# Query heads paired across key heads, and the fourth layer's rotary exchange by transfers inside SBUF

## The reference

```
def rope(x, pos):
    ...
    x1, x2 = jnp.split(xf, 2, axis=-1)
    return jnp.concatenate([x1 * cos - x2 * sin, x2 * cos + x1 * sin], axis=-1).astype(x.dtype)

def swa_mixer(h, w_in, sinks, w_o):
    W, hd, Hq, Hkv = SWA_WINDOW, HEAD_DIM, SWA_Q_HEADS, SWA_KV_HEADS     # 128, 64, 16, 4
    q, k, v = jnp.split(h @ w_in, [Hq * hd, (Hq + Hkv) * hd], axis=-1)
    q, k = rope(q), rope(k)                                               # heads split, positions 0..255
    # query head i uses key head i // 4; a band of 128 keys; a sink column in the softmax
    scores = where(mask, q k^T * hd ** -0.5, -inf)
    probs = softmax([scores, sink])[..., :-1]
    return (probs @ v) @ w_o
```

## Time and profile before

| what | value |
|---|---|
| median of 3 runs | 1587.19 us (1586.34 to 1588.76) |
| profiled execution, its own time | 1587.09 us |
| its span, first to last instruction | 1585.2 us |
| mean granted TensorE clock | 0.992 of full speed |
| layer 4's stage from the first unit pair's end to out_part(7) | about 989 to 1050 us of the span |

### The profile page before, as it was taken

One profiled execution on the slowest core, in us unless ns is written; L12 is line 12 of the kernel. 1 busy time (PEld: TensorE's weight loads), 2 busy tenths in 40 slices (PEclk: granted clock), 3 DMA queues, 4 the chain that ended last, 5 costly groups with the idle time before them and its releaser, 6 DMA issues.

```text
span 1585.2 us, 24605 instructions
## 1 busy us (share of the span) xinstructions
PE 1523.4 (96%) x9396; PEld 1320.1 (83%) x9396; DVE 1202.2 (76%) x1724; ACT 794.6 (50%) x1053; POOL 110.9 (7%) x111
## 2 busy tenths in 40 slices
PE   2989999999999999999999999999999999999999
PEld 1867888889988888899888888787888888889998
DVE  6898877778578777865687777968777788676666
ACT  2455444356464343565543445565434577655544
POOL 0150000000000000011000000220000063200000
PEclk8999999999999999999999999999999999999999
DMA  9855987856258878573478885446888655345550
GB/s 389 360 189 214 370 318 302 307 189 238 81 213 325 331 297 340 197 260 133 160 315 332 307 332 197 148 158 256 338 322 314 230 174 185 119 161 185 185 185 27
DMA packets 54908, 383.78 MB, mean 242 GB/s; under 512 B 6420, under 2 KB 6932, under 8 KB 9264
## 3 DMA queue, kind: packets, MB, share of 16 engines
q1 hardware_dynamic: 50976, 363.75, 60.9%
q0 software_dynamic: 3856, 18.97, 3.4%
HBM read 381.62 MB, written 4.22 MB: 243 GB/s over the span
## 4 chain that ended last, share of the span: by engine, by line
PE 81%; DVE 10%; DMA 3%; issue 3%; ACT 2%; POOL 1%; SPq 0%; DVEq 0%; ACTq 0%
PE PS L2367 27%; PE PS L1977 25%; PE PS L2425 17%; DVE adar L1423 3%; PE PS L1998 3%; DVE wlo L1398 2%; DMA CST<-cst_in 1%; PE PS L2128 1%; PE PS L2178 1%; PE PS L2403 1%; ACT whi L947 1%; DMA adar<-ada 1%; DVE SCR L1585 1%; PE PS L2056 1%; PE PS L2155 1%
## 5 line engine op out<-in xcount | busy, mean ns | idle before, releaser
L1398 DVE TENSOR_TENSOR wlo<-raw,whi 128x2048 fp32r<-128x2048 f32 x229 | 526.4, 2300 | 220.9 <-ACT whi L947 220.6
L947 ACT ACTIVATE whi<-raw 128x2048 fp32r<-128x2048 f32 x234 | 446.3, 1910 | 193.3 <-PE PS L2425 122.6
L1977 PE MATMUL PS<-hhi,whi 128*128 128x256 f32 x1104 | 320.6, 290 | 3.5 <-DVE wlo L1398 2.6
L1977 PE MATMUL PS<-hlo,whi 128*128 128x256 f32 x1104 | 314.5, 285 | 0.0
L1977 PE MATMUL PS<-hhi,wlo 128*128 128x256 f32 x1104 | 314.3, 285 | 0.0
L1423 DVE CUSTOM_DVE_ANT_0 adar<-adar,CB 128x1024 f32<-128x1024 f32 x232 | 277.0, 1234 | 8.4 <-DMA adar<-ada 8.3
L2367 PE MATMUL PS<-whi,hhi 128*128 128x512 f32 x704 | 278.5, 396 | 2.0 <-ACT hhi L996 2.0
L2367 PE MATMUL PS<-wlo,hhi 128*128 128x512 f32 x704 | 274.4, 390 | 0.0
L2367 PE MATMUL PS<-whi,hlo 128*128 128x512 f32 x704 | 274.1, 390 | 0.0
L1977 PEld LDWEIGHTS PS<-hhi,whi 128*128 128x128 f32 x1104 | 213.5, 193 | 11.3 <-issue 7.8
L1977 PEld LDWEIGHTS PS<-hlo,whi 128*128 128x128 f32 x1104 | 213.7, 194 | 1.6 <-issue 1.2
(11 more groups left out here) (259 smaller groups left out, 1993.3 us busy)
## 6 DMA issues: line engine op xcount, KB each, us to landing
raw<-weights SPq DMA_DIRECT2D x234, 1024.0 KB, 6.4
adar<-ada SPq DMA_DIRECT2D x104, 1024.0 KB, 6.2
adar<-ada POOLq DMA_DIRECT2D x12, 1024.0 KB, 5.5
raw<-ada SPq DMA_DIRECT2D x4, 1024.0 KB, 15.1
bias_rows<-bias_of_distance POOLq DMA_DIRECT2D x1, 3072.0 KB, 13.9
adar<-bias_rows POOLq DMA_DIRECT2D x8, 256.0 KB, 3.3
CST<-cst_in SPq DMA_DIRECT2D x1, 1128.0 KB, 22.7
CB<-c_in SPq DMA_DIRECT2D x2, 512.0 KB, 4.0
```

The lines of the kernel that those rows point to most:

```text
L947: act.activation(whi[:, u % CV, :], raw[:, u % RAW, :], ACT.Copy).then_inc(hi_done, 1)
L1398: v.tensor_tensor(wlo[:, u % CV, :], raw[:, u % RAW, :], whi[:, u % CV, :].bitcast(F32), ALU.subtract).then_inc(lo_done, 1)
L1977: m = pe.matmul(o, w(a), h(b), start=first and k_ == 0, stop=last and k_ == 2, skip_group_check=True)
```

## The change

1. The 16 query heads are paired across key heads: pair p holds the heads 8 (p // 4) + p % 4 and that + 4, which belong to the key heads 2 (p // 4) and 2 (p // 4) + 1. The columns of w_in, the rows of w_o and the sinks are put in that order on the host. So a half of the partitions meets only the key head that lies there, and the exchanged copy of KT (L1546) is dropped in both swa layers.
2. In layer 4 alone, the five products with the permutation matrix are dropped. In their place POOL issues, for each rotated unit, four transfers from SCR to the part of KT that has become free (columns 2 to 5, two buffers), each of 32 partitions x 512 elements (64 KB): the partition blocks exchanged two by two. DVE's rotation waits for them, and multiplies and adds in SBUF.
3. values(0) to values(2) of layer 4 no longer wait for rotations 3 to 5, since those products no longer write a bank that values use.

The core of the diff:

```diff
+def swa_heads():
+
+    return [8 * (p // 4) + 4 * h + p % 4 for p in range(PAIRS) for h in range(2)]
...
+        def moved_rotation(kind, l):
+
+            return kind == "swa" and l > 0
...
+        def partners(k):
+
+            return KT[:, 2 + 2 * (k % 2):4 + 2 * (k % 2), :].rearrange("p a b -> p (a b)")
...
+                def load_partners(i):
+
+                    k = aux_units[kind].index(i)
+                    pool.wait_ge(bank_read, reads[l, i])
+                    if k >= 2:
+                        pool.wait_ge(aux_done, aux0[l] + k - 1)
+                    for q in range(4):
+                        dst, source = 32 * q, 32 * (q ^ 1)
+                        pool.dma_start(partners(k)[dst:dst + 32, :], SCR[source:source + 32, k % 2, :]).then_inc(pair_in[k % 2], 16)
...
+                if moved_rotation(kind, l):
+                    for i in (0, 1, 3):
+                        load_partners(i)
                 if kind in ("swa", "fox"):
                     for p in range(PAIRS):
+                        if moved_rotation(kind, l) and p in (1, 2):
+                            load_partners(3 + p)
                         normalise(p)
...
-                    turned = two(SCR[:, 2, :])
-                    v.wait_ge(aux_pe, a + 1)
-                    v.tensor_tensor(rt, rt, bc(cst("cos", S), 2), ALU.mult)
-                    link(v.tensor_tensor(turned, two(aux_bank(kind, k)[:]), bc(cst("sin", S), 2), ALU.mult))
-                    if i:
-                        q = k - 1
-                        v.tensor_tensor(QT[:, 2 * q:2 * q + 2, :], rt, turned, ALU.add).then_inc(aux_done, 1)
+                    if moved_rotation(kind, l):
+                        turned = two(partners(k))
+                        v.wait_ge(pair_in[k % 2], 64 * (k // 2 + 1))
+                        v.tensor_tensor(rt, rt, bc(cst("cos", S), 2), ALU.mult)
+                        link(v.tensor_tensor(turned, turned, bc(cst("sin", S), 2), ALU.mult))
                     else:
-
-                        v.tensor_tensor(KT[:, 0:2, :], rt, turned, ALU.add)
-                        for half in range(2):
-                            other = slice(64 - 64 * half, 128 - 64 * half)
-                            e = v.tensor_tensor(KT[64 * half:64 * half + 64, 2:4, :], rt[other], turned[other], ALU.add)
-                        e.then_inc(aux_done, 1)
+                        turned = two(SCR[:, 2, :])
+                        v.wait_ge(aux_pe, pe0[l] + k + 1)
+                        v.tensor_tensor(rt, rt, bc(cst("cos", S), 2), ALU.mult)
+                        link(v.tensor_tensor(turned, two(aux_bank(kind, k)[:]), bc(cst("sin", S), 2), ALU.mult))
+                    dst = QT[:, 2 * k - 2:2 * k, :] if k else KT[:, 0:2, :]
+                    v.tensor_tensor(dst, rt, turned, ALU.add).then_inc(aux_done, 1)
                     v.wait_ge(aux_done, a + 1)
...
                 def aux_product(i):
 
+                    if moved_rotation(kind, l):
+                        return
...
-                            kt = p // 4 + 2 * ((p // 2 + h) % 2) if kind == "swa" else p
+                            kt = p // 4 if kind == "swa" else p
...
-                        if p < 3:
+                        if p < 3 and not moved_rotation(kind, l):
                             pe.wait_ge(aux_done, aux0[l] + 3 + p)
...
-                                col = HD * (p // 2 if kind == "swa" else 2 * p + h)
+                                col = HD * (2 * (p // 4) + h if kind == "swa" else 2 * p + h)
```

More of the change, by code:

```diff
@@ L233, in program @@
         bank_read = sem("projection_read")
+        pair_in = [sem(f"rotation_partners_loaded{i}") for i in range(2)]
         aux_in, aux_pe, aux_roots, aux_done = sem("aux_squares"), sem("aux_product"), sem("aux_roots"), sem("aux_done")
@@ L324, in program @@
         aux_units = {"swa": [0, 1, 3, 4, 5], "b2": [0, 1, 3, 4, 6, 7, 9, 10]}
-        aux0, total = {}, 0
+        aux0, pe0, total, products = {}, {}, 0, 0
         for l, k in enumerate(kinds):
-            aux0[l] = total
+            aux0[l], pe0[l] = total, products
             total += len(aux_units.get(k, []))
+            products += 0 if moved_rotation(k, l) else len(aux_units.get(k, []))
+        def partners(k):
+            return KT[:, 2 + 2 * (k % 2):4 + 2 * (k % 2), :].rearrange("p a b -> p (a b)")
         def aux_bank(kind, a):
@@ L1043, in square_read @@
                     if k >= 2:
-                        act.wait_ge(aux_pe, aux0[l] + k - 1)
+                        act.wait_ge(aux_pe, pe0[l] + k - 1)
                     act.wait_ge(pe_unit, u0 + i + 1)
@@ L1050, in head_root @@
                     k = aux.index(i)
-                    act.wait_ge(aux_pe, aux0[l] + k + 1)
+                    act.wait_ge(aux_pe, pe0[l] + k + 1)
                     if k >= 2:
@@ L2544, in pack @@
             gains += [i["norm_gain"][src, 0], i["norm_gain"][src, 1]]
+            if kind == "swa":
+                w_in, w_o = w_in.copy(), w_o.reshape(16, HD, D)[swa_heads()].reshape(D, D)
+                w_in[:, 0:D] = w_in[:, 0:D].reshape(D, 16, HD)[:, swa_heads()].reshape(D, D)
         units += [cols(w_in, UC * n, UC) for n in UNIT_ORDER[kind]]
@@ L2575, in pack @@
     put("lam", np.stack([i[n][0] for n in ("lambda_q1_2", "lambda_k1_2", "lambda_q2_2", "lambda_k2_2")], 1), HD)
-    put("sinks", np.broadcast_to(i["swa_sinks"].reshape(1, 32), (P, 32)))
+    put("sinks", np.broadcast_to(i["swa_sinks"][:, swa_heads()].reshape(1, 32), (P, 32)))
     put("bf", i["fox_b_f"][0][:, None], 16)
```

## The result

The changed kernel takes **1601.54 us** (median of 4 runs, 1600.20 to 1602.82), the kernel before 1587.03 beside it (4 runs): a ratio of **1.0089** (95% interval 1.0077 to 1.0101), 14.5 us slower. The forecast was 1592.9, range 1588.8 to 1598.8. The direction was right, the size was not, and the time lies outside the range.

The account below looks back on a forecast made before the run. PE and DVE, both full in layer 4, were taken to bound the kernel. Layer 4's +7.1 and layer 1's -1.4 made +5.7 us, forecasting 1592.9 us, with a range of 1588.8 to 1598.8.

Parts of the forecast that it names:

- What bounds the kernel: Layer 4: PE and DVE are both full, so taking work from PE alone gains nothing while DVE stays late.
- Layer 1, -1.4: Layer 1, first rotation: dropping its two half copies saves 1.4 us, or 0 if DVE meets a late load.
- Layer 4, the first two rotations, +0.9: Layer 4 before scores(0): DVE waits for two groups of transfers, landing 2.7 us after issue, so scores(0) comes 0.9 later.
- The bound of 6.0: Layer 4's first two rotations: slowest transfer landing assumed, 6.0 us, which would put scores(0) 4.2 us later.
- The rule that I drew from the Trainium skill's "TensorE: Matmul & The Clock Gate": Layer 4's three PE waits: each pays a 1.7 us clock drop in full, 5.1 instead of 1.0, giving 1597.0 us.
- Transposes(1), +1.3 beyond scores(0): Layer 4: the fourth rotation's transfers precede normalise(1) in POOL's queue, making transposes(1) about 2.2 us later in all.
- Transposes(2), +4.8 more: Layer 4: PE waits 4.7 us for unit 5's copy, four POOL issues and normalise(2); transposes(2) forecast 7.0 later in all.
- Behind it, +0.1: Layer 4 after transposes(2): fifth product gone -1.0, covered wait -0.4, slower normalise(3) +0.5, clock drop +1.0.
- The sum: Whole kernel: +7.1 us in layer 4 and -1.4 in layer 1, making +5.7.
- The rival of clock and landing: Layer 4: two more clock drops give 1595.4 us, transfers landing after 6.0 give 1596.2, both 1599; chance 0.20.
- double mishap: Layer 4: late landings together with every clock drop, left out of the range, which ended at 1598.8 us.
- The absorbed rival: Layer 4: POOL queueing partly given back, including the last transposes' 1.62 us wait; total +2.0, 1589.1 us; chance 0.16.

Follow-up runs that it names:

- the loads held: Changed kernel with SyncE holding back three groups of its layer 4 loads until a rotation's transfers have landed: 1593.53 us, ratio 1.0041 to the kernel before.
- The filler: Changed kernel plus idle PE products, 8 ahead of scores(0) and 6 ahead of transposes(2): 1598.98 us, ratio 1.0075 to the kernel before.
- no exchange at all: Changed kernel with no transfers issued or waited for, leaving out layer 4's exchange of rotary halves: 1584.12 us, ratio 0.9975 to the kernel before.

## Why the prediction was wrong, by its own steps

**What bounds the kernel: right.** PE and DVE are both full in layer 4. With PE's products taken out for nothing, DVE's chain left 2.7 of their 4.9.

**Layer 1, -1.4: right.** The pairing alone gave 1.5 and 2.3 in two measurements, at most 0.2 of it in layer 4. The changed kernel's layer 4 starts 1.8 earlier, but by itself one such start would not have borne this out. Layer 1's own marks do: scores(0) stands at 65.88 before and at 64.56 and 64.85 in the two pairings, and the transposes that stand at 113.56 before stand at 112.28 and 112.15.

**Layer 4, the first two rotations, +0.9: the step that failed.** It measured +5.9. Its arithmetic stands, since with the loads held the step is +0.1, and 1.9 in place of 2.7 as the landing makes just that. The landing was wrong. I took 2.7 from transfers "in weight traffic", whose traffic was not that of 995 to 1003: the four from 1306 ran beside one load, issued at 1303.46, where here two loads of 1 MB are in flight: 5.4 to 7.7. The bound of 6.0 came from those rows as well, and the last transfer, the one that counts, took 7.74. The Trainium skill's "DMA: Bandwidth & Descriptors", section "Anatomy of one DMA", would have made it 2.15: close to the 1.8 to 1.9 of a lone transfer, far from the one on the path.

**The clock behind scores(0), left out: +2.5.** A wait of 3.6 would have stood there by my own sum, and layer 1's rows showed a drop behind one of 3.26; I put its price in a rival only. The wait of 8.60 brought the clock to 0.50, the one of 2.77 with the loads held did not. A wait's length alone doesn't decide it: there 2.18 at transposes(1) did, with a wait of 1.00 at scores(2) ahead of it, and in the kernel where SyncE issues so did 3.61. The filler shows the price, 2.6. The second drop, where I had +1.0, cost 1.4. The rule that I drew from the Trainium skill's "TensorE: Matmul & The Clock Gate" (it stands in its section "Why this matters for your kernels", not in the one that I named), three waits at 1.7 each, 5.1 in all, is nearer to the measured 4.0 than my 1.0, though a drop followed only two of the three waits.

**Transposes(1), +1.3 beyond scores(0): 0.0.** The group of issues and normalise(1) stood there as I had it, but the copy that they wait for came 1.4 sooner behind scores(1) than before, 9.5 in place of 10.9 on ACT's timeline; I had kept it where it was. PE waits 0.55, after 1.19 at scores(2), which takes up what the products gone from there give. With the loads held, and PE early, the wait is 2.18, as forecast.

**Transposes(2), +4.8 more: right in kind, 2.1 too small.** Measured +6.9. (My own terms end at 1030.6, which is +6.9 in all and not the +7.0 that I wrote.) The wait without slowed normalising is 4.67 and 4.68 in two kernels, against 4.7. The missing 2.1 is normalise(2): 2.68 in place of 0.61, beside DVE's subtraction of a weight unit, which began at 1033.52, just ahead of it. I had seen that price in the earlier trace rows but placed it at normalise(3), and at 0.5 (the same section of the Trainium skill's "SBUF — State Buffer" says that of a GpSimd operation that reads SBUF and a VectorE operation with two inputs there, the one that starts second stands still until the other is done; the 2.1 and DVE's 2.28 agree): where everything shifts by 6 us, what an operation runs beside must be looked up anew.

**Behind it, +0.1: +0.8.** The product and the covered wait (-1.4) balance the clock (+1.4). Normalise(3), where I had +0.5, took 0.4 more (0.97 and 1.48 against 0.97 and 1.04), but PE shows no wait for it. What the 0.8 is made of I did not test.

**The sum.** 16.2 in layer 4, of which the runs show 7.8 for the queue with its clock. The other 8.6 are by subtraction: the landing with its clock, less what the missing products give. Against no exchange at all the same sum is 19.1, so 11.3 for the landing beside 7.8, if the two add, which no run shows. The 8.5 at scores(1) is close to the 8.6, but it is another quantity. Less layer 1's gain, the 16.2 is the 14.5 measured. The rival of clock and landing named both causes and gave 1599 for them together; I cut the range just below that, as a "double mishap". They are not two mishaps: the late landing is what makes the wait that drops the clock. The absorbed rival was wrong: the last wait is there in every kernel, at 1.62 to 1.71.

## What to carry to other kernels

Price a small transfer by the loads that are in flight when it is issued, not by the traffic of the rows that you have: here the same 64 KB took 1.9 or 7.7. If it has to go, put it ahead of the loads and behind what others wait for in its queue. And ask first what the work that it replaces covers: five products of about 1 us, started when their input was ready, were worth 2.7 us at most. The best version here is the pairing alone, 1585.7 and 1586.3, with the products kept.

## What was not expected of the hardware

- A transfer inside SBUF and its landing beside 1 MB loads: 1.8 to 1.9 us alone, 5.4 to 7.7 beside two loads; at 256 KB 2.3 alone and 6.3 to 7.6 beside them.
- Splitting into four costs the issuing queue, not the landing: 0.50 per issue on POOL, 0.59 on SyncE's queue.
- POOL's first half of a normalisation takes 0.61 or 2.6 to 2.7, by what DVE does beside it; here that alone was 2.1 us on the path.
